# A mixer stage in another order: convolution between weight blocks, memory transposes inside the last value block, output projection begun on the convolution's rows

## The reference, cut to what matters

```python
def parallel_mixer(h, w_in, conv_w, lb, hgrn_norm, w_out):
    proj = jnp.einsum('bsd,dp->bsp', h, w_in)
    cb, cc, cx, hq, hf, hi, hg = jnp.split(proj, N_PROJ_SLOTS, axis=-1)
    u = jnp.pad(cc * cx, ((0, 0), (CONV_K - 1, 0), (0, 0)))
    conv = sum(u[:, j:j + seq] * conv_w[j] for j in range(CONV_K))
    y_a = cb * conv
    ...
    log_f = jnp.log(lbh + (1.0 - lbh) * jax.nn.sigmoid(z))     # z: hf by heads
    k = (1.0 - lbh) * jax.nn.sigmoid(-z)
    o = hgrn2_chunkwise(q, k, v, log_f)    # q: hq, v: hi; S_t = diag(f_t) S_{t-1} + k_t v_t^T, o_t = S_t^T q_t
    o = o * lax.rsqrt(jnp.mean(o * o, axis=-1, keepdims=True) + EPS)
    o = o * hgrn_norm.reshape(HGRN_HEADS, HGRN_DV)
    y_b = (o * jax.nn.silu(g)).reshape(bsz, seq, HGRN_WIDTH)   # g: hg by heads
    y = jnp.concatenate([y_a, y_b], axis=-1)
    return jnp.einsum('bsm,md->bsd', y, w_out)

x = x + parallel_mixer(rms_norm_2(x, mix_norm[l]), w_in[l], conv_w[l], lb_all[l], hgrn_norm[l], w_out[l])
x = x + memory_cross_attention(rms_norm_2(x, xattn_norm[l]), rms_norm_2(mem, mem_norm[l]), w_q[l], w_kv[l], w_o[l])
```

## Time and profile before

| | us |
|---|---|
| median of 3 runs | 2027.73 |
| lowest, highest | 2023.18, 2029.29 |
| the profiled execution | 2019.04 |
| its span, first to last instruction | 2017.4 |
| mean granted clock of PE, share of full speed | 0.964 |

### The profile page before, as it was taken

The page is one execution under the profiler, slowest core; times in us unless marked ns, Lnnn a source line. Parts: engine busy times, 40 slices in busy tenths (PEclk is TensorE's granted clock), DMA queues, the critical chain, the costliest instruction groups (busy, mean ns, idle before and its releaser), DMA issues.

```text
span 2017.4 us, 25894 instructions
## 1 busy us (share of the span) xinstructions
PE 1853.8 (92%) x10094; PEld 1580.2 (78%) x10094; DVE 1341.3 (66%) x1876; ACT 910.5 (45%) x967; POOL 76.5 (4%) x99
## 2 busy tenths in 40 slices
PE   5999976999799899999999999888977899999997
PEld 3778744788698679999999999787966678878875
DVE  5688775759897555555555555647953478888885
ACT  2543433411233344444444444445543457666664
POOL 0000000000000331110000000000000000000000
PEclk9999997999899999999999999898988899999999
DMA  6655443434345775666555555544334178888892
GB/s 270 240 178 204 149 144 135 167 108 145 116 148 200 236 239 192 213 206 215 186 187 187 187 187 187 197 155 152 126 117 188 55 293 327 327 343 330 319 350 106
DMA packets 60847, 403.93 MB, mean 200 GB/s; under 512 B 7921, under 2 KB 8337, under 8 KB 14305
## 3 DMA queue, kind: packets, MB, share of 16 engines
q1 hardware_dynamic: 51504, 371.22, 50.6%
q0 software_dynamic: 5808, 20.29, 3.4%
q10 hardware_dynamic: 3458, 11.37, 1.7%
HBM read 390.79 MB, written 12.06 MB: 200 GB/s over the span
## 4 chain that ended last, share of the span: by engine, by line
PE 82%; DVE 9%; ACT 3%; issue 3%; DMA 3%; SPq 0%; ACTq 0%; DVEq 0%
PE ps L2152 21%; PE ps L2153 21%; PE ps L2154 21%; PE ps L2254 7%; PE ps L2530 3%; ACT whi L630 2%; DVE wlo L1125 2%; DMA raw<-in_stream_dram 1%; DMA X<-in_x_dram 1%; PE ps L2702 1%; PE ps L2767 1%; PE ps L2589 1%; PE ps L2183 1%; PE ps L2397 1%; PE ps L2629 1%
## 5 line engine op out<-in xcount | busy, mean ns | idle before, releaser
L1125 DVE TENSOR_TENSOR wlo<-raw,whi 128x2048 fp32r<-128x2048 f32 x186 | 429.6, 2310 | 394.0 <-ACT whi L630 394.0
L630 ACT ACTIVATE whi<-raw 128x2048 fp32r<-128x2048 f32 x186 | 356.2, 1915 | 395.0 <-PE ps L2154 372.1
L2152 PE MATMUL ps<-thi,whi 128*128 128x256 f32 x1088 | 310.6, 285 | 9.5 <-DVE wlo L1125 7.0
L2153 PE MATMUL ps<-tlo,whi 128*128 128x256 f32 x1088 | 309.9, 285 | 0.0
L2154 PE MATMUL ps<-thi,wlo 128*128 128x256 f32 x1088 | 309.8, 285 | 0.0
L2152 PE MATMUL ps<-whi,phi 128*128 128x512 f32 x608 | 242.9, 400 | 21.9 <-DVE plo L1705 15.6
L2152 PE MATMUL ps<-whi,thi 128*128 128x512 f32 (+1 forms) x584 | 232.5, 398 | 20.1 <-DVE tlo L1137 11.7
L2153 PE MATMUL ps<-wlo,phi 128*128 128x512 f32 x608 | 240.8, 396 | 0.0
L2154 PE MATMUL ps<-whi,plo 128*128 128x512 f32 x608 | 239.9, 395 | 0.0
L2154 PE MATMUL ps<-whi,tlo 128*128 128x512 f32 (+1 forms) x584 | 228.4, 391 | 0.0
L2153 PE MATMUL ps<-wlo,thi 128*128 128x512 f32 (+1 forms) x584 | 228.1, 391 | 0.0
(11 more groups left out here) (403 smaller groups left out, 2624.2 us busy)
## 6 DMA issues: line engine op xcount, KB each, us to landing
raw<-in_stream_dram SPq DMA_DIRECT2D x264, 1024.0 KB, 4.8
BIG<-in_stream_dram SPq DMA_DIRECT2D x83, 1024.0 KB, 7.0
...
g_spill<-H ACTq DMA_DIRECT2D x4, 1024.0 KB, 4.8
g_spill<-MOD ACTq DMA_DIRECT2D x4, 1024.0 KB, 4.8
...
```

What stands on the lines that cost most here:

```text
L630: nc.scalar.activation(whi[:, u % 2, :], raw[:, u % 2, :], ACT.Copy).then_inc(unit_hi, 1)
L1125: nc.vector.tensor_tensor(wlo[:, u % 2, :], raw[:, u % 2, :], whi[:, u % 2, :].bitcast(f32), ALU.subtract).then_inc(unit_split, 1)
L2152: nc.tensor.matmul(out, ahi, bhi, start=start, stop=False)
L2153: nc.tensor.matmul(out, ahi, blo, start=False, stop=False)
```

## The change

On DVE the first mixer units' `lo` go ahead of the masks and of the memory's norm, and the masks, `lb` and the norm stand one by one between later units. The convolution (which needs mixer units 0 to 5 alone) stands between `lo` of mixer units 8 to 11 and not behind all of them; `conv_plo` stands ahead of the scan, and `lo` of unit 13 behind the scan and the first exponents. On ACT the small Exp and the memory's norm move in between the mixer units 1 to 5; `conv_phi` and the first level's Abs and Exp go ahead of `hi` of key/value unit 0; the evacuation of hg goes behind level 2's Exp. On PE the transposes of `T_MEM` stand between mixer units 12 and 13 (four banks, two chunks of all tokens each), `split_rows(T_MEM)` goes, key/value unit 0 waits chunk pair by chunk pair and stands ahead of level 0, and level 1 follows level 0 at once. At the end of the stage output unit 0 starts behind the recurrence's output on the rows of the convolution, with the transposes of `T_YB` behind each of its two token tiles; the norm is made tile by tile, its squares and its product read PSUM, the product with `hgrn_norm` goes to level 7, and `hi`/`lo` of output unit 1 go behind it. The numbers of computed values stay the same.

```diff
         def tr_place(t, k, first=0):
...
+            if t == T_MEM:
+                return slice(2 * k, 2 * k + 2), slice(0, S)
```

```diff
             for u in range(MIX_T):
                 hi(U_MIX + u + 2)
                 evac(N_MT + u, U_MIX + u, mixT[:, 2 * u:2 * u + 2, :].rearrange("p b t -> p (b t)"))
+                if u == 1:
+                    act.wait_ge(small_logs, 2)
+                    nc.scalar.activation(lb, lb, ACT.Exp).then_inc(small_exps, 1)
+                if u == 3:
+                    norm(3, mem, mem_loaded, (16, 16))
...
             for t in range(TT):
                 evac(N_MV + t, U_MIX + MIX_T + 1, hv[:, t, :])
-            hi(U_KV)
-            hi(U_KV + 1)
-            for t in range(TT):
-                evac(N_MV + 2 + t, U_MIX + MIX_T + 3, hg[:, t, :], ACT.Silu)
             act.wait_ge(conv_ready, 1)
             nc.scalar.activation(conv_phi, conv_y, ACT.Copy).then_inc(conv_hi, 1)
-            tr_high(T_MEM)
+
+            def level_exp(l):
+
+                act.wait_ge(lev_d, l)
+                mark(nc.scalar.activation(lev_e[l % 2], lev_e[l % 2], ACT.Abs))
+                settle()
+                nc.scalar.activation(lev_e[l % 2], lev_e[l % 2], ACT.Exp, scale=-1.0).then_inc(lev_exp, 1)
+
+            level_exp(1)
+            hi(U_KV)
+            used(U_MIX + MIX_T + 2)
+            tr_high(T_MEM, groups=(0, 1))
+            used(U_MIX + MIX_T + 3)
+            tr_high(T_MEM, groups=(2, 3))
+            hi(U_KV + 1)
+            level_exp(2)
+            for t in range(TT):
+                evac(N_MV + 2 + t, U_MIX + MIX_T + 3, hg[:, t, :], ACT.Silu)
...
-            for l in range(1, LEVELS + 2):
-                act.wait_ge(lev_d, l)
-                mark(nc.scalar.activation(lev_e[l % 2], lev_e[l % 2], ACT.Abs))
-                settle()
-                nc.scalar.activation(lev_e[l % 2], lev_e[l % 2], ACT.Exp, scale=-1.0).then_inc(lev_exp, 1)
-                if l >= 2:
-                    memory(l - 2)
-                    hi(U_KV + l)
+            for l in range(2, LEVELS + 2):
+                if l > 2:
+                    level_exp(l)
+                memory(l - 2)
+                hi(U_KV + l)
+            root_table()
             memory(LEVELS)
+            for t in range(TT):
+                act.wait_ge(ro_full, t + 1)
+                nc.scalar.activation(ro[:, t, :], ps[:, 4 + t, :], ACT.Square).then_inc(ro_sq, 1)
+                act.wait_ge(ro_ms, t + 1)
+                nc.scalar.activation(r_stat[:, t * RH:(t + 1) * RH], r_stat[:, t * RH:(t + 1) * RH],
+                                     ACT.Sqrt).then_inc(ro_std, 1)
             hi(U_KV + LEVELS + 2)
-            for t in range(TT):
-                act.wait_ge(ro_full, t + 1)
-                nc.scalar.activation(ro[:, t, :], ps[:, 4 + t, :], ACT.Copy).then_inc(ro_copied, 1)
-            act.wait_ge(ro_copied, TT)
-            nc.scalar.activation(lev_q.rearrange("p b t -> p (b t)"), ro.rearrange("p t n -> p (t n)"),
-                                 ACT.Square).then_inc(ro_sq, 1)
-            act.wait_ge(ro_ms, 1)
-            nc.scalar.activation(r_stat[:, 0:TT * RH], r_stat[:, 0:TT * RH], ACT.Sqrt).then_inc(ro_std, 1)
```

On DVE:

```diff
             lo(U_MIX + 1)
+            lo(U_MIX + 2)
...
+            lo(U_MIX + 3)
+            dve.wait_ge(mix_loaded, 48)
+            nc.vector.tensor_tensor(lb, lb2[:, RH:2 * RH], lb2[:, 0:RH], ALU.subtract).then_inc(small_logs, 1)
             for l in range(LEVELS):
...
-            dve.wait_ge(mix_loaded, 48)
-            nc.vector.tensor_tensor(lb, lb2[:, RH:2 * RH], lb2[:, 0:RH], ALU.subtract).then_inc(small_logs, 1)
+            lo(U_MIX + 4)
...
+            lo(U_MIX + 5)
             norm(3, mem, rows_ready)
-            for u in range(MIX_T):
-                lo(U_MIX + u + 2)
-
-            dve.wait_ge(z_sig, 2)
-            settle()
...
-            lo(U_MIX + MIX_T + 2)
-
-            dve.wait_ge(acc_free, N_MT + MIX_T)
-            mark(nc.vector.tensor_tensor(conv_u, cc, cx, ALU.mult))
-            settle()
-            for j in (2, 1, 0):
+
...
-                if j == 2:
-                    lo(U_MIX + MIX_T + 3)
+
+            lo(U_MIX + 6)
+            lo(U_MIX + 7)
+            lo(U_MIX + 8)
+            dve.wait_ge(acc_free, N_MT + 6)
+            mark(nc.vector.tensor_tensor(conv_u, cc, cx, ALU.mult))
+            conv_tap(2)
+            lo(U_MIX + 9)
+            conv_tap(1)
+            lo(U_MIX + 10)
+            conv_tap(0)
+            settle()
             nc.vector.tensor_tensor(conv_y, conv_y, cb, ALU.mult).then_inc(conv_ready, 1)
-
+            lo(U_MIX + 11)
+
+            dve.wait_ge(z_sig, 2)
...
+            lo(U_MIX + MIX_T + 2)
+
+            dve.wait_ge(conv_hi, 1)
+            nc.vector.tensor_tensor(conv_plo, conv_y, conv_phi.bitcast(f32), ALU.subtract).then_inc(conv_lo, 1)
             dve.wait_ge(f_log, 1)
...
-                dve.wait_ge(lev_full, l)
+                if l >= 2:
+                    dve.wait_ge(lev_full, l)
...
             exponents(1)
+            lo(U_MIX + MIX_T + 3)
+            exponents(2)
+            decayed(1)
             lo(U_KV)
+            tr_low(T_MEM)
             lo(U_KV + 1)
-            tr_low(T_MEM)
-            for l in range(1, LEVELS + 2):
+            collect(0)
+            for l in range(2, LEVELS + 2):
                 if l <= LEVELS:
                     exponents(l + 1)
                 decayed(l)
                 collect(l - 1)
-                if l == 1:
-                    dve.wait_ge(conv_hi, 1)
-                    nc.vector.tensor_tensor(conv_plo, conv_y, conv_phi.bitcast(f32), ALU.subtract).then_inc(conv_lo, 1)
-                else:
-                    lo(U_KV + l)
+                if l == LEVELS:
+                    mark(nc.vector.tensor_tensor(hg, hg, hnorm.unsqueeze(1).broadcast_to([P, TT, CW]), ALU.mult))
+                lo(U_KV + l)
             collect(LEVELS + 1)
-            lo(U_KV + LEVELS + 2)
-
-            dve.wait_ge(ro_sq, 1)
-            rst = r_stat[:, 0:TT * RH]
-            mark(nc.vector.tensor_reduce(rst, lev_q.rearrange("p b t -> p (b t)").rearrange("p (h d) -> p h d", d=P),
-                                         axis=AX.X, op=ALU.add))
-            mark(nc.vector.tensor_tensor(hg, hg, hnorm.unsqueeze(1).broadcast_to([P, TT, CW]), ALU.mult))
-            root_mean(rst, P, (dve_chain, chain[0]), ro_ms, ro_std, 1)
-            rov = ro.rearrange("p t (h d) -> p (t h) d", d=P)
-            mark(nc.vector.tensor_tensor(rov, rov, rst.unsqueeze(2).broadcast_to([P, TT * RH, P]), ALU.mult))
-            settle()
-            for t in range(TT):
+
+            for t in range(TT):
+                rst = r_stat[:, t * RH:(t + 1) * RH]
+                rows = ro[:, t, :].rearrange("p (h d) -> p h d", d=P)
+                dve.wait_ge(ro_sq, t + 1)
+                mark(nc.vector.tensor_reduce(rst, rows, axis=AX.X, op=ALU.add))
+                settle()
+                nc.vector.tensor_scalar(rst, rst, 1.0 / P, EPS, ALU.mult, ALU.add).then_inc(ro_ms, 1)
+                dve.wait_ge(ro_std, t + 1)
+                mark(nc.vector.reciprocal(rst, rst))
+                settle()
+                mark(nc.vector.tensor_tensor(rows, ps[:, 4 + t, :].rearrange("p (h d) -> p h d", d=P),
+                                             rst.unsqueeze(2).broadcast_to([P, RH, P]), ALU.mult))
+                settle()
                 nc.vector.tensor_tensor(H[:, t, 0:CW], ro[:, t, :], hg[:, t, :], ALU.mult).then_inc(rows_ready, 1)
             tr_low(T_YB, 4)
+            lo(U_KV + LEVELS + 2)
```

On PE:

```diff
                 group_T(N_MT + u, U_MIX + u, T_MIX if u == 0 else None)
-            for b in range(2):
-                block_rows(N_MV + 2 * b, U_MIX + MIX_T + 2 * b)
+            block_rows(N_MV, U_MIX + MIX_T)
+            block_rows(N_MV + 2, U_MIX + MIX_T + 2, units=(0,))
             transposes(T_MEM, H)
-            split_rows(T_MEM)
+            block_rows(N_MV + 2, U_MIX + MIX_T + 2, units=(1,))
+            group_T(N_K, U_KV, T_MEM)
 
             for l in range(LEVELS + 2):
                 qs, ks = (hq, rk) if l == 0 else (lev_q, lev_k)
                 if l == 0:
-                    pe.wait_ge(acc_free, N_K)
-                    pe.wait_ge(conv_ready, 1)
+                    pe.wait_ge(lev_d, 1)
                 else:
                     pe.wait_ge(lev_qk, l)
                     if l >= 2:
...
                 last.then_inc(lev_full, 1)
-                if l < 4:
+                if 1 <= l < 4:
                     group_T(N_K + l, U_KV + l)
-                elif l < 8:
...
+            for t in range(TT):
+                rows_part(N_W2, U_WO2, 0, t, source=mixed_rows)
+                transposes(T_YB, H, (t,))
+            for t in range(TT):
+                pe.wait_ge(tr_lo, T_BASE[T_YB] + t + 1)
+                rows_part(N_W2, U_WO2, 1, t, source=mixed_rows)
+            block_rows(N_W2 + 2, U_WO2 + 2, source=mixed_rows, ends=True)
 
 
             transposes(T_HX, H)
```

(9 more changed lines are left out.)

47 lines of the change are left out of this document (30 added, 17 removed).

## The result

The changed kernel took 2009.48 us (median of 4, 2003.05 to 2011.04) against 2028.33 for the kernel before beside it (4 runs, 2023.18 to 2029.29): 18.9 us less. The forecast was 2008.1 and 19.6 us less.

A forecast was written before the change was run, and what follows sets the result against it. PE bounds the kernel, with its stops in the mixer stage and the clock lost behind them. 8.1 + 4.7 - 0.3 + 7.1 = 19.6 us takes the median from 2027.73 to 2008.1, range 2002 to 2017.

The forecast's parts named there:

- Term 1: First mixer units: `hi` and `lo` ahead of masks and norm let unit 2 start without waiting; 8.1 us gained.
- the stop behind the norm: Mixer stage: the moved norm makes the next `hi` 1.6 late against 1.5 of slack, a stop of 0.1 us.
- SP's loads follow `lo`; those of the first units come no later: First mixer units: the moved work delays none of SP's loads, so it costs nothing.
- Term 2: `T_MEM` and first levels: level 1 starts earlier despite a new stop before unit 13; 4.7 us gained.
- The stop before unit 13: Mixer unit 13 waits for its `lo` behind DVE's convolution, scan and exponents: a new stop of 3.6 us.
- rival 3: `lo` of unit 13 and of output unit 1 come in time; gains grow by 0.3 and 3.7, 2004.1; chance 0.06.
- that rule: Before key/value unit 0: a drain of about 1.38 us behind the added table load makes the sum 1.1 smaller.
- The level of `hgrn_norm`: Level 7: the product with `hgrn_norm` (1.22) pushes `lo` back by 1.2; 0.3 us lost.
- Term 3: Tail: PE goes from the recurrence's output into output unit 0 at once, new stop before output unit 1; 7.1 gained.
- The clock behind the stops: PE's clock falls behind the new stops before mixer unit 13 and output unit 1, at 1.5 us each.
- Rivals 1 to 4: Alternatives; the second: unit 2 stays gated, 2016.2, chance 0.05; the last: low clock through all levels, up to 2060, chance 0.03.
- rival 1: Mixer stage and tail: cover of the moved norm or the clock is worse; gain 13.6, 2014.1; chance 0.17 for 10 to 16.

The follow-up runs named there:

- alone 7.7: The kernel before with only the order of the first mixer units changed; 2020.05 us, ratio 0.9943 to the kernel before.

## Why the prediction came out right, point by point

**The sum.** 18.54 us measured in the stage, 19.6 forecast; all four terms are within 0.4 us of their forecast.

**Term 1** (8.1, measured 7.74; alone 7.7). Unit 2 starts at once, as worked out. What is missing is the stop behind the norm: 0.37 with its slow first matmul, where I had 0.1. `hi` came 1.4 late (1338.32 and not 1336.90) where I had 1.6, but the reserve was 1.1 and not 1.5. The prediction took the start of the next `hi` (1342.38 before the change) for the time at which PE wants `lo`; PE's next matmul is due 0.25 before that (0.12 behind the last one, `hi` 0.37), and in the change it started 0.15 behind the end of `lo` (1342.54, 1342.69). The step "SP's loads follow `lo`; those of the first units come no later" left out the load behind the norm, whose `lo` came late. It had no price, neither here nor where it held a `hi` by 1.1 us.

**Term 2** (4.7, measured 4.35). The stop before unit 13 was to be 3.6 and is 3.84, and the clock behind it took 1.7 and not 1.5; the two make the 0.4. DVE's order is the one foreseen:

```profile
1380.83 1.23 DVE L1840 TENSOR_TENSOR plo<-BIG,phi 128x1024 fp32r<-128x1024 f32 x1 [4.38 <-ACT phi L961]
1381.97 2.43 DVE L1843 TENSOR_TENSOR_SCAN BIG<-MID,BIG 128x256 f32<-128x256 f32 x4
1384.44 1.23 DVE L1856 TENSOR_TENSOR BIG<-BIG 128x1024 f32<-128x1024 f32 x1
1385.58 2.28 DVE L1146 TENSOR_TENSOR wlo<-raw,whi 128x2048 fp32r<-128x2048 f32 x1
```

`wlo` ends at 1387.86, PE starts at 1387.92. The claim that key/value unit 0 also waits for level 1's Exp, so that an early `lo` of unit 13 brings almost nothing (0.3 in rival 3), was borne out by the run that moved that `lo` alone; it even cost 1.3, since the clock now fell later, over key/value unit 0.

The table load of this path is at 1386.77 in ACT's timeline:

```profile
1386.77 1.28 ACT L968 ACT_TABLE_LOAD   x1
1388.07 1.06 ACT L968 ACTIVATE BIG<-BIG 128x1024 f32<-128x1024 f32 x1
1389.03 1.90 ACT L640 ACTIVATE whi<-raw 128x2048 fp32r<-128x2048 f32 x1
```

The Exp starts 0.02 us behind the load's end. The drain that the Trainium skill names (ScalarE: Activation LUTs, What ACT_TABLE_LOAD costs) is again not seen, and the sum by the rows was the nearer one: the path from mixer unit 11 on was to gain 4.7 by them, 3.6 by that rule, and gained 4.35. The run that moved `lo` of unit 13 alone tells it apart more sharply, since there this chain alone held key/value unit 0. It starts 17.9 us behind `hi` of mixer unit 13 (1379.32, 1397.24); the prediction has 17.8 by the rows and would have 19.1 by the rule.

**The level of `hgrn_norm`:** -0.35 against -0.3.

**Term 3** (7.1, measured 6.79). The stop is 3.70 as forecast, and no transpose of `T_YB` waits. The clock took 1.7 and not 1.5.

**The clock behind the stops.** Both stops lost it, as taken from the stop of 3.27 in the earlier trace rows. The windows of the change around both:

```profile
1386.00:1388.00 2.00, 0.08 (x1) 0.08 (x1) 2.00 (x2) 1.98 (x2) 0.00 (x0) 1.00 0.02 4
1388.00:1390.00 2.00, 2.00 (x6) 1.58 (x7) 1.84 (x2) 1.99 (x3) 0.00 (x0) 0.66 0.44 82
1390.00:1392.00 2.00, 2.00 (x6) 1.56 (x5) 1.97 (x3) 1.90 (x3) 0.00 (x0) 0.50 0.97 406
1392.00:1394.00 2.00, 2.00 (x10) 1.60 (x10) 2.00 (x2) 0.00 (x0) 0.00 (x0) 0.99 0.09 37
...
1470.00:1472.00 2.00, 2.00 (x7) 1.53 (x8) 1.92 (x1) 0.00 (x0) 0.00 (x0) 0.64 0.49 115
1472.00:1474.00 2.00, 2.00 (x6) 1.62 (x5) 0.00 (x0) 0.00 (x0) 0.00 (x0) 0.51 0.98 414
```

A PEclk of 0.50 is the lower level, 1.2 GHz. Six matmuls pass in such a window and ten at 2.4 GHz. About 3.4 us at the lower level cost 1.7 each time.

**The profiled execution.** Here the prediction was wrong: 1999.4 was forecast and it took 2010.63. I took everything outside the stage as fixed. It moves by several us from one execution to the next, as the repeats of both kernels show, so the forecast for a single execution needed a range of its own. The difference of the medians, which averages this, was right. Rivals 1 to 4 don't show: the cover of the norm was short, as in rival 1, but by 0.3 us and without a fall of the clock; no stop stands before unit 2 or at the levels, and both stops of rival 3 stand.
